# Layer 0's modulation in four 32-column tiles of TensorE, and its fourth unit in two pieces

## The chip, the core and the metric

The kernel runs on one core of a Trainium2 chip. The metric is the device time of one execution in microseconds (us). TensorE (PE) multiplies, VectorE (DVE), ScalarE (ACT) and GpSimd (POOL) do the rest, and SyncE (SP) issues most loads from the chip's memory (HBM). Each engine runs its own list of instructions in order and waits on semaphores.

## What is computed

Two decoder layers on 256 tokens of width 1024, in float32. The part that matters here is how layer 0 begins.

```python
c_act = jax.nn.silu(c)
for i in range(DEPTH):
    mod = c_act @ ada_w[i] + ada_b[i]
    sh1, sc1, g1, sh2, sc2, g2 = jnp.split(mod[:, None, :], 6, axis=-1)
    h = rms_norm(x, norm_mix[i]) * (1.0 + sc1) + sh1
    ...
    y = dilated_attention(h, attn_w_qkv[a], attn_w_out[a], ...)   # layer 0; layer 1: hgrn2_mixer
    x = x + g1 * y
    h = rms_norm(x, norm_ffn[i]) * (1.0 + sc2) + sh2
    x = x + g2 * swiglu(h, ffn_w1[i], ffn_w3[i], ffn_w2[i])
```

c is one row of 1024, ada_w[0] is 1024x6144. Of `mod` the first product needs sh1 and sc1, 2048 columns.

## The kernel before

**Products in three parts.** Weights come in units of 128x2048 (1 MB) into a ring of six slots, `raw`. ACT rounds a unit to the reduced form F32R (`whi`, `round_unit`), DVE writes the rest over the slot (`wlo`, `split_unit`), and PE adds three products: activation high x weight high, low x high, high x low. The activations stand transposed in `hT` (8 blocks of 128 columns of the model, 256 tokens), their rounded form in `hT_hi`, the rest in `hT_lo`.

**The start.** Layer 0's first six units are done by `half_unit(m)`: m is 0 to 2 with the first four blocks of hT (half 0) and 3 to 5 with the last four (half 1). So units 0 to 2 need the modulation of half 0 alone: for each half, 512 columns of sh1 and 512 of sc1. A unit is six runs of four 128x512 products: high and low part against `whi` for both tiles of tokens t, then high against `wlo` for both.

**The modulation.** ada_w's columns of a half come in eight chunks `first_w[k]`, one for 128 rows, 128x1024 each; `first_load(n)` loads chunk n, with n = 8 to 15 for half 1, into the same eight places. `first_sum(blk, k)` on DVE multiplies chunk k by the column `cact[:, k]` and adds it up in `acc[:, blk]`. PE then sums `acc` over the partitions by eight products with a column of ones (`first_reduce`); of half 0 the last chunk goes to PE directly, by eight one-column products. `first_modulation(half)` on DVE adds the bias and makes the gain `mod_a`, `first_affine(half, t)` makes h of hT in place, ACT rounds it (`first_round`), DVE makes the low part (`first_rest`).

**What sets the order.** The lists of all engines are written out by hand. SP's loads before: c, chunks 0 and 1, x, chunks 2 to 7, unit 0 in two pieces, chunk 8, unit 1, chunks 9 to 12, unit 2, chunks 13 to 15, unit 3 and on. `keep_clock(n)` runs n products whose result nobody reads, 128x512 in float32, in between (fillers, below). DVE's list for half 1 has the sums of all eight chunks around the splits of units 1 and 2. `bank[i]` are the eight banks of PSUM, where PE writes; a float32 product stands in the trace as two records with a weight load each, a float32 transpose as one.

## Time and profile before

| | us |
|---|---|
| median of 3 runs (lowest, highest) | 870.5 (870.15, 871.99) |
| the profiled execution, its own time | 872.44 |
| its span, first to last instruction | 870.6 |
| PE busy | 839.7 (96%) |
| DVE busy | 613.9 (71%) |
| ACT busy | 432.6 (50%) |
| POOL busy | 137.9 (16%) |

The times in all rows are microseconds from the start of the span, of one execution. A row of a timeline has the start, the busy time, the engine (PEld is PE's load of weights), the line, the operation, what it writes and reads, partitions x elements, and how many records it merges; in brackets the idle time ahead of it and what ended it. The end of a record of PE is modelled: it lies some 0.17 behind the end of its stream.

### The profile page before, as it was taken

Reading aid. Unit: us, or ns where it says so; the run is one execution under the profiler, and the core shown is the slowest. Engines: PE = TensorE matmul, PEld = TensorE weight load, DVE = VectorE, ACT = ScalarE, POOL = GpSimd, SP = SyncE. Lnnn points to the kernel's source line nnn. Section 1 sums busy time; section 2 is a strip of 40 time slices with the busy share of each in tenths; the row PEclk is TensorE's granted clock in tenths of the full one; section 3 lists DMA queues with packets and bytes.
Section 4 is the critical chain, followed back from the end, with each engine's and each line's share of the span. In section 5 each row is a group of like instructions: output and inputs, shape, how many; then the busy total and the mean of one; then the engine's idle time right before and its main releaser. Section 6 shows DMA issues by size and latency. Waiting matters only on the chain.

```text
span 870.6 us, 10955 instructions
## 1 busy us (share of the span) xinstructions
PE 839.7 (96%) x4254; PEld 699.8 (80%) x4254; DVE 613.9 (71%) x728; ACT 432.6 (50%) x549; POOL 137.9 (16%) x157
## 2 busy tenths in 40 slices
PE   4999999999999989999999989999999999999998
PEld 2778878878878878887888877888888788887886
DVE  4897798788888776577576676787867665654544
ACT  5355464464445555453344356778575744433431
POOL 3000101111010120011010020467813000000000
PEclk9799999999999999999999999999999999999999
DMA  9997878887877635688787745434234577665521
GB/s 320 365 357 238 293 253 276 283 255 234 284 260 235 229 108 193 198 275 293 260 271 255 240 145 180 156 98 146 97 117 129 208 248 234 228 206 180 192 96 49
DMA packets 122102, 188.97 MB, mean 217 GB/s; under 512 B 5683, under 2 KB 91048, under 8 KB 122052
## 3 DMA queue, kind: packets, MB, share of 16 engines
q1 hardware_dynamic: 109796, 146.10, 51.8%
q0 software_dynamic: 12256, 42.18, 14.4%
q8 instruction: 34, 0.56, 0.3%
q14 instruction: 16, 0.13, 0.0%
HBM read 187.18 MB, written 1.09 MB: 216 GB/s over the span
## 4 chain that ended last, share of the span: by engine, by line
PE 76%; DVE 13%; ACT 4%; issue 4%; DMA 2%; POOL 1%; SPq 0%; DVEq 0%; ACTq 0%; POOLq 0%
PE bank L526 62%; DVE wlo L1363 2%; PE bank L642 2%; DVE acc L1374 2%; DVE x L1532 2%; PE bank L722 2%; PE bank L748 1%; PE bank L916 1%; ACT whi L988 1%; PE bank L595 1%; PE bank L703 1%; PE bank L860 1%; DMA x<-in_x_dram 1%; PE bank L559 1%; DVE sq L1530 1%
## 5 line engine op out<-in xcount | busy, mean ns | idle before, releaser
L1363 DVE TENSOR_TENSOR wlo<-raw,whi 128x2048 fp32r<-128x2048 f32 x123 | 285.4, 2325 | 41.9 <-ACT whi L988 41.8
L988 ACT ACTIVATE whi<-raw 128x2048 fp32r<-128x2048 f32 (+1 forms) x124 | 235.3, 1900 | 18.9 <-DMA raw<-in_attn_w_qkv_dram 12.2
L526 PE MATMUL bank<-whi,hT_hi 128*128 128x512 f32 (+1 forms) x728 | 195.1, 391 | 2.4 <-ACT hT_hi L988 1.5
L526 PE MATMUL bank<-wlo,hT_hi 128*128 128x512 f32 (+1 forms) x752 | 194.1, 381 | 1.2 <-DVE wlo L1363 1.2
L526 PE MATMUL bank<-whi,hT_lo 128*128 128x512 f32 (+1 forms) x728 | 187.3, 380 | 0.0
L526 PEld LDWEIGHTS bank<-wlo,hT_hi 128*128 128x128 f32 x752 | 137.3, 188 | 29.5 <-DVE wlo L1363 2.0
L526 PEld LDWEIGHTS bank<-whi,hT_lo 128*128 128x128 f32 x728 | 132.9, 188 | 26.5
L526 PEld LDWEIGHTS bank<-whi,hT_hi 128*128 128x128 f32 x728 | 129.5, 188 | 29.9 <-issue 6.5
L393 POOL DMA_DIRECT2D ada_w<-in_ada_w_dram x80 | 42.7, 534 | 466.2 <-DVE acc L1374 449.0
L1374 DVE SCALAR_TENSOR_TENSOR acc<-ada_w,cact,acc 128x1024 f32<-128x1024 f32 x80 | 102.3, 1279 | 8.0 <-DMA ada_w<-in_ada_w_dram 6.0
L1224 ACT ACTIVATE arena<-bank 128x256 f32<-128x256 f32 x44 | 14.5, 381 | 166.8 <-PE bank L526 166.8
L1686 DVE TENSOR_TENSOR arena<-bank,arena 128x256 f32<-128x256 f32 x44 | 16.6, 419 | 112.2 <-ACT arena L1224 112.2
L526 PE MATMUL bank<-whi,oT_hi 128*128 128x512 f32 x240 | 70.3, 410 | 0.0
L526 PE MATMUL bank<-wlo,oT_hi 128*128 128x512 f32 x240 | 65.9, 392 | 0.0
L526 PE MATMUL bank<-whi,oT_lo 128*128 128x512 f32 x240 | 65.5, 390 | 0.0
L526 PEld LDWEIGHTS bank<-wlo,oT_hi 128*128 128x128 f32 x240 | 45.6, 190 | 10.1
L526 PEld LDWEIGHTS bank<-whi,oT_lo 128*128 128x128 f32 x240 | 45.1, 188 | 9.7
L526 PEld LDWEIGHTS bank<-whi,oT_hi 128*128 128x128 f32 x240 | 43.8, 192 | 8.0 <-issue 0.5
L988 ACT ACTIVATE oT_hi<-bank 128x512 fp32r<-128x512 f32 (+1 forms) x38 | 17.6, 464 | 58.4 <-PE bank L748 39.0
L988 ACT ACTIVATE arena<-bank 128x512 f32<-128x512 f32 (+3 forms) x63 | 30.0, 528 | 20.4 <-PE bank L526 9.2
L1131 ACT ACTIVATE arena<-arena,small 128x768 f32<-128x768 f32 (+1 forms) x16 | 12.5, 779 | 35.4 <-DVE small L1609 23.9
L399 POOL TENSOR_TENSOR wlo<-raw,spare 128x2048 fp32r<-128x2048 f32 x3 | 14.2, 4748 | 76.0 <-ACT spare L988 76.0
(184 smaller groups left out, 854.5 us busy)
## 6 DMA issues: line engine op xcount, KB each, us to landing
raw<-in_ffn_w_dram SPq DMA_DIRECT2D x88, 512.0 KB, 4.9
ada_w<-in_ada_w_dram POOLq DMA_DIRECT2D x80, 512.0 KB, 5.0
raw<-in_attn_w_qkv_dram SPq DMA_DIRECT2D x62, 512.0 KB, 6.5
raw<-in_ffn_w_dram SPq DMA_DIRECT2D x22, 1024.0 KB, 4.9
raw<-in_hgrn_w_in_dram SPq DMA_DIRECT2D x16, 1024.0 KB, 5.4
arena<-in_ada_w_dram SPq DMA_DIRECT2D x16, 512.0 KB, 10.1
raw<-in_attn_w_qkv_dram SPq DMA_DIRECT2D x4, 1024.0 KB, 7.1
raw<-in_attn_w_out_dram SPq DMA_DIRECT2D x4, 1024.0 KB, 7.4
```

What stands on the lines that cost most here:

```text
L393: pool.dma_start(ada_w[:, n % ADA_RING], a["ada_w"][layer, k * P:(k + 1) * P, b * ADA_COLS:(b + 1) * ADA_COLS]).then_inc(ada_in[n % ADA_RI ...
L399: pool.tensor_tensor(wlo[:, m % RAW, :], raw[:, m % RAW, :], hi_of(m).bitcast(F32), ALU.subtract).then_inc(s["split_second"], 1)
L526: mm = nc.tensor.matmul(dst[t][c][:, 0:n], lhs[:, k0 + k, t * P:(t + 1) * P], w[:, k, c * 512:c * 512 + n], start=start and k == 0, stop=s ...
L642: mm = nc.tensor.matmul(bank[b + t][:], lhs[:, 4 * half + k, t * P:(t + 1) * P], w[:, k, :], start=start and half == 0 and k == 0, stop=st ...
L722: mm = nc.tensor.matmul(dst, qT[:, pr % 2, g, base + qt * P:base + (qt + 1) * P], kT[:, pr % 2, g, base:base + w], start=True, stop=True)
L988: return nc.scalar.activation(dst, src, ACT.Copy)
L1131: nc.scalar.activation(pr_, pr_, ACT.Exp, bias=stat(J, 2), accum_out=stat(J, 3)).then_inc(s["att_p"], 1)
L1224: i = nc.scalar.activation(sil[:, t], gate_bank(j, t)[:, 0:FC], ACT.Silu)
L1363: nc.vector.tensor_tensor(wlo[:, m % RAW, :], raw[:, m % RAW, :], fp(hi_of(m)), ALU.subtract).then_inc(s["split"], 1)
L1374: nc.vector.scalar_tensor_tensor(out=acc[:, blk % 2], in0=ada_w[:, n % ADA_RING], scalar=cact[:, k:k + 1], in1=acc[:, blk % 2], op0=ALU.mu ...
L1532: nc.vector.tensor_tensor(x[:, t, cut], x[:, t, cut], sq[:, b % 2], ALU.add).then_inc(s["res"], 1)
L1686: i = nc.vector.tensor_tensor(hid[:, t], gate_bank(j, t)[:, FC:2 * FC], sil[:, t], ALU.mult)
```

## The change

**Sums.** Each chunk of half 0, and chunks 5 to 7 of half 1 (`SUMMED = 5`), are summed by PE: `quarters` runs four products with 32 stationary columns, all equal (`cact32`, the column of c's activation repeated 32 times, written once by DVE into a free part of `acc`), and 256 moving columns of the chunk, with outputs on partitions 0, 32, 64 and 96 of one bank. The bank adds up over the chunks. For half 1 DVE still sums chunks 0 to 4 in `acc`, and `quarters` adds that with a stationary of ones. Then DVE copies the 128x256 result to `acc`, PE transposes it in two pieces (`first_columns`), and DVE adds the bias.

**Fillers** read ones instead of x, and stand between the chunks. There are three after chunk 1, one each after chunks 2, 4 and 5 (here behind the transposes) and others, and two behind each `first_columns`.

**Unit 3** comes and is rounded in two pieces; in its products the split's run of tile 0 is moved ahead of the low part of tile 1. **Half 1's h**: DVE writes `hT_hi` of tile 0 directly and then makes h in place; ACT does both for tile 1 (`second_half_tile`).

**Order of loads**: unit 2 ahead of chunks 11 and 12; a place of a chunk is free when PE has read it (`first_mm`), not DVE. POOL's zeroing of `acc` for the next block waits for the second modulation.

```diff
@@ SP
                 blk, k = divmod(n, KC)
-                if blk and k == KC - 1:
-                    sp.wait_ge(s["first_mm"], 1)
-                elif blk:
-                    sp.wait_ge(s["first_sum"], k + 1)
+                if blk:
+                    sp.wait_ge(s["first_mm"], k + 1)
...
             first_load(KC)
             load_unit(1)
-            for n in range(KC + 1, KC + 5):
+            first_load(KC + 1)
+            first_load(KC + 2)
+            load_unit(2)
+            for n in range(KC + 3, 2 * KC):
                 first_load(n)
-            load_unit(2)
-            for n in range(KC + 5, 2 * KC):
-                first_load(n)
-            for m in range(3, UNITS):
+            load_by_halves(3)
+            for m in range(4, UNITS):
@@ PE
+            def quarters(dst, left, right, start, stop):
+
+                for r in range(4):
+                    mm = nc.tensor.matmul(dst[32 * r:32 * r + 32, 0:256], left, right[:, r * 256:(r + 1) * 256],
+                                          start=start, stop=stop)
+                return mm
+
+            def first_chunk(n, start=False, stop=False):
+
+                half, k = divmod(n, KC)
+                pe.wait_ge(first_in[n], 16)
+                mm = quarters(bank[7 if half else 3], cact32[:, k, :], first_w[k], start, stop)
+                mm.then_inc(s["first_mm"], 1)
+
+            def first_columns(half, dst):
+
+                pe.wait_ge(s["mod_copy"], half + 1)
+                for i in range(2):
+                    mm = nc.tensor.transpose(dst[:, 256 + i * P:256 + (i + 1) * P], acc[:, half, i * P:(i + 1) * P], ident[:])
+                mm.then_inc(s["mod_red"], 1)
...
+                if m == 3:
+                    pe.wait_ge(s["split"], m + 1)
+                    product(hT_hi, w[1], 0, False, True)
+                    pe.wait_ge(s["xn_lo"], 2 * half + 2)
+                    product(hT_lo, w[0], 1, False, False)
+                    product(hT_hi, w[1], 1, False, True).then_inc(s["pe_unit"], 1)
+                    return
                 pe.wait_ge(s["xn_lo"], 2 * half + 2)
                 product(hT_lo, w[0], 1, False, False)
                 if m == 2:
-                    first_reduce(1, bank[7])
+                    first_chunk(KC + SUMMED, start=True)
                 pe.wait_ge(s["split"], m + 1)
                 product(hT_hi, w[1], 0, False, True)
+                if m == 2:
+                    for k in range(SUMMED + 1, KC - 1):
+                        first_chunk(KC + k)
+                    pe.wait_ge(s["first_sum"], SUMMED)
+                    quarters(bank[7], ones[:, 0:32], acc[:, 1], False, False)
                 product(hT_hi, w[1], 1, False, True).then_inc(s["pe_unit"], 1)
+                if m == 2:
+                    first_chunk(2 * KC - 1, stop=True)
+                    first_columns(1, bank[7])
+                    keep_clock(2, 6)
@@ DVE
             def first_modulation(half):
 
+                b = bank[7 if half else 3]
+                dve.wait_ge(s["first_mm"], 2 * KC - SUMMED if half else KC)
+                nc.vector.tensor_copy(acc[:, half, 0:256], b[:, 0:256]).then_inc(s["mod_copy"], 1)
                 dve.wait_ge(s["mod_red"], half + 1)
...
-            for k in range(2, KC):
+            first_sum(1, 2)
+            first_sum(1, 3)
+            split_unit(2)
+            for k in range(4, SUMMED):
                 first_sum(1, k)
-            split_unit(2)
             first_modulation(1)
+            cut = slice(0, P)
+            for kc in range(4, KC):
+                i = nc.vector.tensor_scalar(hT_hi[:, kc, cut], hT[:, kc, cut], mod_a[:, 0, 0, kc:kc + 1],
+                                            first_shift(kc), ALU.mult, ALU.add)
+            i.then_inc(s["xn_hi"], 1)
             first_affine(1, 0)
-            first_affine(1, 1)
+            dve.wait_ge(s["h0_aff"], 3)
             first_rest(1, 0)
+            split_unit(3)
             first_rest(1, 1)
-            split_unit(3)
```

PE's list before, from the transpose of the small rows to the first product. L610 is the filler, L559 the transposes of the normalised x, L624 the table of position biases, L628 the last chunk, L603 the sum over the partitions.

```order
L616 MATMUL bank<-ident,rows 128x79
L610 MATMUL bank<-x,ident 128x512 x2
L559 MATMUL bank<-ident,arena 128x128 x8
L610 MATMUL bank<-x,ident 128x512
L559 MATMUL bank<-ident,arena 128x128 x8
L624 MATMUL bank<-arena 24x383
L610 MATMUL bank<-x,ident 128x512
L628 MATMUL bank<-cact,arena 128x1 x8
L603 MATMUL bank<-ones,acc 128x1 x8
L610 MATMUL bank<-x,ident 128x512
```

The same place after the change. L606 is `quarters`, 4 for a chunk, L627 the filler, L563 the transposes, L650 the table, L621 `first_columns`.

```order
L606 MATMUL bank<-arena,acc 32x256 x4
L627 MATMUL bank<-ones,ident 128x512
L606 MATMUL bank<-arena,acc 32x256 x4
L563 MATMUL bank<-ident,arena 128x128 x8
L627 MATMUL bank<-ones,ident 128x512
L606 MATMUL bank<-arena,acc 32x256 x4
L627 MATMUL bank<-ones,ident 128x512
L606 MATMUL bank<-arena,acc 32x256 x4
L563 MATMUL bank<-ident,arena 128x128 x8
L627 MATMUL bank<-ones,ident 128x512
L606 MATMUL bank<-arena,acc 32x256 x4
L650 MATMUL bank<-arena 24x383
L627 MATMUL bank<-ones,ident 128x512
L606 MATMUL bank<-arena,acc 32x256 x4
L621 MATMUL bank<-ident,acc 128x128 x2
```

From chunk 2 to chunk 7 the list now has five fillers between the transposes, the table and six groups of quarters, where it had two fillers and one chunk.

PE's list at the end of unit 2 before, with the sum over partitions between the low-part run and the `wlo` runs:

```order
L642 MATMUL bank<-whi,hT_hi 128x512 x4
L642 MATMUL bank<-whi,hT_lo 128x512 x4
L603 MATMUL bank<-ones,acc 128x1 x8
L642 MATMUL bank<-wlo,hT_hi 128x512 x8
L642 MATMUL bank<-whi,hT_hi 128x512 x4
```

And after the change:

```order
L664 MATMUL bank<-whi,hT_hi 128x512 x4
L664 MATMUL bank<-whi,hT_lo 128x512 x4
L606 MATMUL bank<-arena,acc 32x256 x4
L664 MATMUL bank<-wlo,hT_hi 128x512 x4
L606 MATMUL bank<-arena,acc 32x256 x4
L606 MATMUL bank<-acc,ones 32x256 x4
L664 MATMUL bank<-wlo,hT_hi 128x512 x4
L606 MATMUL bank<-arena,acc 32x256 x4
L621 MATMUL bank<-ident,acc 128x128 x2
L627 MATMUL bank<-ones,ident 128x512 x2
```

The two `wlo` runs now stand ahead of the last sum.

## Rows read from the trace of the kernel before

**Rows 1.** The page's head and first part: busy time of each engine.
```profile
span 870.6 us, 10955 instructions
PE 839.7 (96%) x4254; PEld 699.8 (80%) x4254; DVE 613.9 (71%) x728; ACT 432.6 (50%) x549; POOL 137.9 (16%) x157
```

**Rows 2.** Stretches: busy time of each engine, granted clock, DMA share, GB/s.
```profile
core 0: us, PE busy (x) PEld busy (x) DVE busy (x) ACT busy (x) POOL busy (x), PEclk, DMA share, GB/s
15.00:21.80 6.80, 6.38 (x40) 4.24 (x38) 5.97 (x11) 4.76 (x8) 0.00 (x0) 1.00 1.07 369
21.80:32.00 10.20, 9.54 (x29) 7.03 (x29) 6.80 (x15) 4.12 (x4) 1.50 (x2) 0.50 1.07 369
32.00:48.50 16.50, 16.08 (x80) 13.28 (x78) 15.59 (x19) 4.47 (x3) 1.09 (x2) 1.00 1.09 361
46.50:67.10 20.60, 19.31 (x87) 15.19 (x85) 20.26 (x31) 13.39 (x18) 0.00 (x0) 1.00 1.07 349
```

**Rows 3.** Timeline of PE, 10.9 to 22.
```profile
10.93 3.70 PE L610 MATMUL bank<-x,ident 128*128 128x512 f32 x4
...
18.79 1.12 PE L610 MATMUL bank<-x,ident 128*128 128x512 f32 x2
19.76 1.84 PE L628 MATMUL bank<-cact,arena 128*128 128x1 f32 x16
21.55 3.37 PE L603 MATMUL bank<-ones,acc 128*128 128x1 f32 x16
```

**Rows 4.** Timeline of PE, from the first unit to the second stage.
```profile
27.49 2.04 PE L642 MATMUL bank<-whi,hT_hi 128*128 128x512 f32 x4 [0.66 <-ACT hT_hi L988]
...
35.19 1.07 PE L642 MATMUL bank<-whi,hT_hi 128*128 128x512 f32 x4
36.10 1.07 PE L642 MATMUL bank<-whi,hT_lo 128*128 128x512 f32 x4
...
40.63 1.07 PE L642 MATMUL bank<-whi,hT_hi 128*128 128x512 f32 x4
...
44.26 1.84 PE L603 MATMUL bank<-ones,acc 128*128 128x1 f32 x16
...
48.46 1.17 PE L642 MATMUL bank<-whi,hT_hi 128*128 128x512 f32 x4 [0.42 <-ACT hT_hi L988]
...
67.13 1.18 PE L526 MATMUL bank<-whi,hT_hi 128*128 128x512 f32 x4 [0.89 <-DVE arena L1587]
```

**Rows 5.** Timeline of DVE, 46.1 to 67.1.
```profile
46.14 0.17 DVE L1402 TENSOR_TENSOR small<-bank,cols 128x8 f32<-128x8 f32 x1 [0.24 <-PE bank L603]
...
46.54 2.14 DVE L1411 TENSOR_SCALAR arena<-arena,mod_a,small 128x128 f32<-128x128 f32 x8
...
65.78 1.29 DVE L1587 TENSOR_TENSOR arena<-bank,small 128x512 f32<-128x512 f32 x2
```

**Rows 6.** Timeline of all engines: arrivals, the first affine, splits and roundings.
```profile
5.11 0.75 DVE L1383 TENSOR_SCALAR acc<-arena,cact 128x1024 f32<-128x1024 f32 x1 [5.11 <-DMA arena<-in_ada_w_dram]
10.01 1.06 ACT L1033 ACTIVATE sq<-x 128x1024 f32<-128x1024 f32 x1 [5.87 <-DMA x<-in_x_dram]
19.33 0.19 PEld L628 LDWEIGHTS bank<-cact,arena 128*128 128x128 f32 x1 [0.24 <-DMA arena<-in_ada_w_dram]
25.57 2.14 DVE L1411 TENSOR_SCALAR arena<-arena,mod_a,small 128x128 f32<-128x128 f32 x8
29.01 2.28 DVE L1363 TENSOR_TENSOR wlo<-raw,whi 128x2048 fp32r<-128x2048 f32 x1
42.64 1.92 ACT L988 ACTIVATE whi<-raw 128x2048 fp32r<-128x2048 f32 x1 [5.81 <-DMA raw<-in_attn_w_qkv_dram]
```

**Rows 7.** Timeline of PE around products with few stationary columns.
```profile
17.62 0.49 PE L559 MATMUL bank<-ident,arena 128*128 128x128 f32 x3
18.04 0.82 PE L624 MATMUL bank<-arena 99*24 99x383 f32 x2
...
590.25 0.70 PE L911 MATMUL bank<-arena 128*32 128x32 f32 x32
...
596.54 1.15 PE L911 MATMUL bank<-arena 128*64 128x64 f32 x16
```

**Rows 8.** Groups by line, DVE: busy, mean ns of one, idle before.
```profile
L1686 DVE TENSOR_TENSOR arena<-bank,arena 128x256 f32<-128x256 f32 x44 | 16.6, 419 | 112.2 <-ACT arena L1224 112.2
```

More of the change, by code:

```diff
@@ L309, in load_unit, with load_by_halves @@
                     sp.dma_start(slot[:, :, c0:c0 + n], src).then_inc(raw_in[m % RAW], 16)
+            def load_by_halves(m):
+                for k in range(0, 4, 2):
+                    for src, nk, c0, n in pieces(m):
+                        slot = raw[:, m, :].rearrange("p (k n) -> p k n", k=nk)
+                        sp.dma_start(slot[:, k:k + 2, c0:c0 + n], src[:, k:k + 2, :]
+                                     ).then_inc(raw_in[m] if k else s["half3_in" if m else "half_in"], 16)
             sp.dma_start(rows[0:KC, :], a["c"].rearrange("a (k d) -> (a k) d", d=P)).then_inc(s["c_in"], 16)
@@ L625, in _ @@
             keep_clock(1)
-            pe.wait_ge(first_in[KC - 1], 16)
-            for j in range(KC):
-                mm = nc.tensor.matmul(bank[3][:, KC + j:KC + j + 1], first_w[KC - 1][:, j * P:(j + 1) * P],
-                                      cact[:, KC - 1:KC], start=True, stop=True)
-            mm.then_inc(s["first_mm"], 1)
-            first_reduce(0, bank[3])
-            keep_clock(1)
+            first_chunk(7, stop=True)
+            first_columns(0, bank[3])
+            keep_clock(2)
             def half_unit(m):
@@ L1076, in _, with round_halves, second_half_tile, affine @@
             copy(tabT, bank[2][0:GH, 0:TABLE]).then_inc(s["tab_cp"], 1)
[L1077 to L1080 removed]
+            def round_halves(m):
+                act.wait_ge(s["half3_in" if m else "half_in"], 32)
+                copy(whi[:, m, 0:UNIT // 2], raw[:, m, 0:UNIT // 2]).then_inc(s["half_rounded"], 1)
+                act.wait_ge(raw_in[m], 32)
+                copy(whi[:, m, UNIT // 2:], raw[:, m, UNIT // 2:]).then_inc(s["rounded"], 1)
+            def second_half_tile():
+                def affine(dst, kc):
+                    return nc.scalar.activation(dst[:, kc, P:2 * P], hT[:, kc, P:2 * P], ACT.Identity,
+                                                bias=first_shift(kc), scale=mod_a[:, 0, 0, kc:kc + 1])
+                act.wait_ge(s["mod_ev"], 2)
+                for kc in range(4, KC):
+                    i = affine(hT_hi, kc)
+                i.then_inc(s["h0_aff_s"], 1)
+                act.wait_ge(s["h0_aff_s"], 1)
+                act.wait_ge(s["xn_hi"], 3)
+                for kc in range(4, KC):
+                    i = affine(hT, kc)
+                i.then_inc(s["xn_hi"], 1)
+            round_halves(0)
             first_round(0, 0)
@@ L1084, in _ @@
             round_unit(2)
-            round_unit(3)
-            first_round(1, 0)
-            first_round(1, 1)
+            round_halves(3)
+            second_half_tile()
             def qk_square(n):
@@ L1547, in _ @@
                                     ).then_inc(s["lbd_s"], 1)
-            for k in range(4, KC - 1):
-                first_sum(0, k)
             first_modulation(0)
```

83 lines of the change are left out of this document (38 added, 45 removed).

## The prediction, written before the kernel was run

> **What bounds the kernel now.** I read the page's first part first: TensorE (PE) is busy for 96% of the span [rows 1]. So most of what is saved or lost before the stream of products runs full reaches the end. Then I read the stretches of the first 48.5 us [rows 2], the products of PE [rows 3, 4] and VectorE (DVE) after the second modulation [rows 5]. Four things are to be seen.
>
> First, PE does no product of the layer before 27.49. It waits for the modulation of the first half: the last chunk of ada_w is there at 19.33 (the L628 weight load waits for its DMA), the eight one-column products L603, behind DVE's last sum, run from 21.55 to 24.9, DVE's small steps lead to the first affine at 25.57, and ScalarE's (ACT) rounding of the result releases PE at 27.49 [rows 3, 4, 6].
>
> Second, the granted clock is 0.50, the 1.2 GHz level, from 21.8 to 32.0, and 1.00 on both sides [rows 2]. In the last 2 us before it fell PE ran one-column products, which stream next to nothing [rows 3]. A run of four 128x512 products takes 0.91 at the full clock (35.19 to 36.10). The first unit, six such runs, takes 7.70 (27.49 to 35.19), the second 5.44 (to 40.63) [rows 4].
>
> Third, the second half: PE reaches the one-column sums L603 at 44.26, DVE has its small steps at 46.14, the first affine at 46.54, PE starts the fourth unit at 48.46 [rows 4, 5].
>
> Fourth, from 46.54 DVE never rests: affines, differences, five splits, two reductions, two normalisations, back to back to 67.07 (busy 20.26 of 20.60), and PE waits for the last of these at 67.13, 0.9 of it idle [rows 2, 4, 5]. So it is **the moment of the second half's first affine**, 46.54, that sets the stretch behind it, and the sum below is made for that moment. The loads are no bound of it: they run without a pause [rows 2], but unit 3 is there at 42.64 [rows 6] and is needed at 48.
>
> **Part 1, what one group of quarters costs.** The new unit of work is four fp32 products with 32 stationary columns and 256 moving ones, to four 32-partition pieces of a bank. A 128x512 fp32 product is two records of 0.43 (a filler: two records, 0.86) [rows 3], so a quarter is two of 0.213. One after the other the eight records are 1.71 us. Do the tiles run together? The trace has one place with 32-column tiles: the 16 products L911, whose outputs alternate between partitions 0 and 64. Their 32 records take 0.70 us with the last one's end, 22 ns each, where the 64-column form of the same line, one tile only, takes 72 ns a record (1.15 for 16) [rows 7]. A record of 32 columns streams 27 ns (0.427 x 32/512), so two tiles overlapped fully. I take the same for four: 2 x 0.213 and some 0.05 for weights and stagger, 0.48.
>
> To this comes the change of form. The table product L624 is the one small-column product between wide ones. Its first record starts 0.20 after the last transpose (three from 17.62 at 0.11 each put that at 17.84), whose stream is 0.05: 0.15 of entry. Its two records stream 0.64 (383 columns), to 18.68, the filler starts at 18.79, and takes 0.97 instead of 0.86: 0.2 of exit [rows 3, 7]. A **group between wide work is 0.15 + 0.48 + 0.20 = 0.83**. The ends: 0.48, if no change of form is paid, and 2.1, if the tiles do not overlap (1.71 + 0.05 + 0.35).
>
> The Trainium skill ("TensorEngine Tiling (Array Packing)", Key Properties) says that changing the tiling mode drains TensorE. The 0.15 before L624 agrees. This rule speaks against this change: it brings nine more such changes in and out. By the skill's "TensorE: Matmul & The Clock Gate" (Part 3) four tiles would start some 4 ns apart, which would make the group 0.79 and the sum 0.4 us lower; no row here has four tiles.
>
> **Part 2, the first half.** Chunk 0 is there at 5.11 [rows 6], chunk 1 a little behind. The quarters of both, three fillers (0.85 a record at the low clock) [rows 3] and the transpose of the small rows fill PE from 5.1 to about 11.5, with the clock risen on the way, as it had before by the filler at 18.79 (0.43 a record). The first chunk that counts, chunk 2, comes at 11.56: x was there at 10.01, chunk 7 at 19.33, so one in 1.55 us [rows 3, 6]. Behind it PE has, in order: six groups 6 x 0.83 = 5.0 (less the last exit 0.2, and 0.35 as chunk 6 and the table product follow each other in the narrow form), five fillers 4.3, sixteen transposes 1.8, the table product with its exit 0.86, and about 0.3 of waiting for chunk 3. 11.5 + 11.7 = **23.2**. So PE, not the DMA, becomes the bound: chunk 7 is 3 us old when it is summed. That is the cost of the fillers once real work shares the queue.
>
> Then the new tail: 0.2 to DVE (L603's end at 46.10 to L1402 at 46.14, and 0.17 of drain), the copy of 256 columns 0.4 (L1686 has 0.42 at this size), 0.5 for two transposes with their weight load, 0.04, two small steps of 0.2 [rows 4, 5, 8]: 1.55. First affine at 24.75 against 25.57: **0.8 gained**. ACT is ready: the table's copy and the two roundings of unit 0 (half of a 1.92 rounding each, [rows 6]) end near 24.5, and it is asked at 25.8. The first product is at 26.7. The four sums and the reduction that DVE loses were not what it waited on last; they free 8 us of DVE, which it spends idle.
>
> **Part 3, the clock.** PE is now full from 11.5 to 26.4 (two fillers cover the tail), with streams and not one-column products in its list, so I let the clock stay at 2.4 GHz. The first unit is then 5.44 and 0.25 for its split: DVE's rest and split end 3.8 after PE's start as before (27.49 to 31.29) [rows 4, 6], PE asks at 3.63. That saves 2.0 of the 7.70. PE is through four of unit 2's six runs at 26.7 + 5.7 + 5.44 + 3.63 = **41.5**, against 44.26: 2.8 earlier.
>
> **Part 4, the second half.** Here the change spends it. Before, 1.7 of L603 and 0.2 led to DVE. Now PE has, on the path: chunk 5 of the half 0.83, a run of wlo 0.91, chunk 6 0.83, the summed chunks 0.45 (same form, no change), a run of wlo 0.91, chunk 7 0.63 without exit: 4.56, to 46.05. The tail 1.55: first affine at **47.6 against 46.54, 1.06 later**. The two wlo runs stood behind the sums before, beside DVE's work; now they stand ahead of it, and two fillers stand beside DVE. DVE's five sums are done by about 41 and hide; before, DVE had all eight to add here. The loads hide: unit 2 is moved ahead of two chunks, which come by about 37, and chunk 7 by 40, all before PE asks.
>
> **Part 5, behind it.** Writing the rounded half straight from DVE saves ACT's step on the way: PE starts the fourth unit 1.15 after the first affine, 1.92 before (48.46) [rows 4]. But DVE must still make the second four affines and the difference (some 2.9), so PE waits about 0.9 for the low part, and 0.45 for the split: the unit ends about 8.0 after the first affine against 7.8 before. DVE's own list to 67.07 has the same entries: same length, 20.5. Unit 3 in two pieces costs nothing and gives nothing, as it is there 5 us early. GpSimd's memset and the ring of ada_w start 3 us later and are first needed beyond 67. So all is 1.06 later: sum 870.5 + 1.1 = **871.6**. The profiled execution had 872.4 with a span of 870.6 [rows 1], the median of the three runs is 870.5: I add the shift to the median.
>
> Each 0.1 on the group moves the end by 0.9 (six groups, then three).
>
> **Rivals.**
> A, the queue stalls on a tile: the second record of a quarter waits for the first and holds up the next tile behind it. Then a group takes five slots of 0.218, 1.44 with its changes, and the added one 0.87. Six times 0.61 in the first half, 3 x 0.61 + 0.42 in the second, 0.4 from the early chunks: 6.4 more, **878**. It decides the sign from a group of 0.9 on. L911's 22 ns speaks against it, but it has two tiles only. With no overlap at all (2.1) it is 886.
> B, faster: the change of form is free and only the streams count, 0.48. PE then waits for chunks 2 and 3, the first affine is at 23.6, the second half's at 45.5: 1.05 gained, **869.4**. If ACT or DVE also lose waits behind it (PE's 0.9 at 67.13) or the tail is 0.5 shorter, 868.5. L624's gaps speak against it.
> C, the clock falls all the same between 12 and 32, since quarters and transposes stream less than full products: 2.3 or more lost in one stretch, **874**.
> D, the relief of DVE is no relief, and nothing else moves: the forecast itself. That the sum is done on PE and off DVE is seen in the order; it can't fail to be done.
>
> **How the numbers follow.** Forecast 0.55, A with its worse form 0.15, B 0.2, C 0.1. The forecast's own range, for groups of 0.7 to 1.0, is 870.3 to 873.2. The range given is 868.2 to 876.5: B and C whole, A outside. What a measurement of this kernel can tell from no change is about 0.2%, 1.7 us. Of the forecast's 0.55 about two thirds lie within it. Faster 0.17, same 0.40, slower 0.43.
>
> **What would show it.** Right: quarters' records at under 60 ns apart, chunk 7's group ending near 23, products from 26.7 at clock 1.00, first affine of the second half near 47.6 with PE full from 41 to 46 and DVE idle before it, then 20.5 us of unbroken DVE. Wrong: groups of 1.1 or more (A), a clock of 0.50 after 12 (C), DVE with gaps between 47 and 67 (then Part 5 fails), or PE waiting for chunks (B).

## The result, and the profile after

| | before | after |
|---|---|---|
| median of 5 (lowest, highest), us | 870.5 (870.15, 871.99) | 875.7 (871.2, 876.58) |
| ratio with its 95% interval | | 1.0045 (1.0029 to 1.0061) |
| the profiled execution, its own time | 872.44 | 871.2 |
| its span | 870.6 | 869.4 |

The changed kernel is slower, by 3.9 us by the ratio and by 5.2 between the medians, where 1.1 was forecast. The range held the time, the likeliest value was 4.1 too low. (One execution each of two kernels below, half1 and keep_after, ran at a mean granted clock of 0.56 and took 1422 and 1435 us; they are left out.) And the profiled execution of the changed kernel is shorter than that of the kernel before, while its median is longer. One execution of each would have shown the change as a gain.

The page's head and first part for the changed kernel, to set beside [rows 1]:

```profile
span 869.4 us, 11083 instructions
PE 842.1 (97%) x4320; PEld 692.3 (80%) x4320; DVE 603.0 (69%) x720; ACT 435.0 (50%) x556; POOL 137.7 (16%) x157
```

DVE has lost 10.9 us of work and PE has gained 2.4, and neither tells what the end did. So I went by the moments that the prediction names. Timeline of PE from chunk 0 to the first product (L606 quarters, L627 filler, L563 transposes, L650 the table, L621 the two transposes of the sum), to set beside [rows 3]:

```profile
5.05 1.08 PE L606 MATMUL bank<-arena,acc 128*32 128x256 f32 x8 [2.63 <-DMA arena<-in_ada_w_dram]
...
11.87 0.64 PE L606 MATMUL bank<-arena,acc 128*32 128x256 f32 x8
12.44 1.13 PE L627 MATMUL bank<-ones,ident 128*128 128x512 f32 x2
13.50 0.64 PE L606 MATMUL bank<-arena,acc 128*32 128x256 f32 x8
14.07 1.09 PE L563 MATMUL bank<-ident,arena 128*128 128x128 f32 x8
...
22.29 0.64 PE L606 MATMUL bank<-arena,acc 128*32 128x256 f32 x8
23.48 0.44 PE L621 MATMUL bank<-ident,acc 128*128 128x128 f32 x2 [0.55 <-DVE acc L1450]
23.75 1.89 PE L627 MATMUL bank<-ones,ident 128*128 128x512 f32 x4
26.27 1.17 PE L664 MATMUL bank<-whi,hT_hi 128*128 128x512 f32 x4 [0.63 <-ACT hT_hi L1026]
```

The four tiles do run together: eight records, two to a quarter, are over in 0.64 with the last one's modelled end, and within the group the first records of the four quarters start 6 to 7 ns apart (13.500, 13.506, 13.513, 13.520). The next wide operation starts 0.57 behind the group's first record (13.50 to 14.07), and a group behind a filler starts 0.20 later than the filler's stream of 0.86 ends (12.44 to 13.50). So a group costs 0.77.

Timeline of PE in the second half, to set beside [rows 4]:

```profile
41.26 0.64 PE L606 MATMUL bank<-arena,acc 128*32 128x256 f32 x8
41.83 1.20 PE L664 MATMUL bank<-wlo,hT_hi 128*128 128x512 f32 x4
42.95 0.64 PE L606 MATMUL bank<-arena,acc 128*32 128x256 f32 x8
43.41 0.61 PE L606 MATMUL bank<-acc,ones 128*32 128x256 f32 x8
43.95 1.19 PE L664 MATMUL bank<-wlo,hT_hi 128*128 128x512 f32 x4
45.08 0.64 PE L606 MATMUL bank<-arena,acc 128*32 128x256 f32 x8
...
68.02 1.20 PE L530 MATMUL bank<-whi,hT_hi 128*128 128x512 f32 x4 [0.86 <-DVE arena L1645]
```

And of DVE: the copy of the sum, which it waits 5.44 for, and the first affine (L1619), to set beside [rows 5]:

```profile
45.78 0.42 DVE L1450 COPY acc<-bank 128x256 f32<-128x256 f32 x1 [5.44 <-PE bank L606]
46.74 0.17 DVE L1456 TENSOR_TENSOR small<-bank,cols 128x8 f32<-128x8 f32 x1 [0.53 <-PE bank L621]
...
47.13 1.23 DVE L1619 TENSOR_SCALAR hT_hi<-arena,mod_a,small 128x128 fp32r<-128x128 f32 x4
```

The second half's first affine is at 47.13 against 46.54, and the seventh unit starts at 68.02 against 67.13 [rows 4, 5]: 0.89 later. That is nearly what the sum said (1.06). From that start to PE's last product this execution takes 797.1. The changed kernel's other timed executions have spans of 872.6 to 874.8 and a mean granted clock of 0.991 to 0.995, where the profiled one has 1.000. So the missing time had to be looked for in executions that the first profile did not show.

### The profile page after: what moved, and what is told of

It reads as the page before. It is cut to its first block, busy times and chain, and to the rows that moved or that the text cites. A ratio compares the mean times of both kernels' runs of the same rounds, so it can differ in the third digit from the quotient of the medians.

```text
span 869.4 us, 11083 instructions
## 1 busy us (share of the span) xinstructions
PE 842.1 (97%) x4320; PEld 692.3 (80%) x4320; DVE 603.0 (69%) x720; ACT 435.0 (50%) x556; POOL 137.7 (16%) x157
## 4 chain that ended last, share of the span: by engine, by line
PE 77%; DVE 12%; ACT 4%; issue 4%; DMA 1%; POOL 1%; SPq 0%; DVEq 0%; ACTq 0%; POOLq 0%
PE bank L530 61%; PE bank L664 3%; DVE wlo L1420 2%; DVE acc L1431 2%; DVE x L1586 2%; PE bank L786 1%; ACT whi L1026 1%; PE bank L760 1%; PE bank L954 1%; PE bank L599 1%; PE bank L898 1%; PE bank L627 1%; PE bank L741 1%; DVE sq L1584 1%; DMA ada_w<-in_ada_w_dram 1%
```

## The experiments

**The changed kernel again, and three edits on its start.** First the changed kernel once more, then single parts of it taken out.

again: no edit.

> The changed kernel once more, nothing altered. Its first profile had TensorE's granted clock at 1.00 over the whole span and 869.4 us; its other runs took 872.6 to 874.8 at a mean clock of 0.991 to 0.995. Theory (clock): the spread over its runs is stretches at the low clock, so the span again follows the mean clock, some 869 at 1.00 and 874 to 875 at 0.991, and the profile shows stretches at 0.50 where TensorE has gaps. Rival (something else, loads or DVE): spans differ by 3 us or more at the same mean clock.

nofill:

```diff
             first_chunk(2)
-            keep_clock(1)
             first_chunk(3)
...
             first_chunk(4)
-            keep_clock(1)
             first_chunk(5)
```

(and three more, all that stand between chunk 2 and chunk 7).

> The changed kernel without the five fillers between chunk 2 and chunk 7 (the three after chunk 1 and those behind the transposes of the sums stay). Theory (the fillers delay the sum): TensorE is done with chunk 7 near 19.9 instead of 22.9, the first affine comes near 21.5, the first product at 24.3, where the rounding of unit 0 ends (it waits for its loads), 2 us earlier than 26.3, and all of it reaches the end if the clock stays: 2 us faster. Rival (they are needed for the clock): the granted clock falls to 0.50 before or in the first units, which costs 2 us or more, and it is the same or slower.

behind:

```diff
-                product(hT_hi, w[1], 1, False, True).then_inc(s["pe_unit"], 1)
                 if m == 2:
                     first_chunk(2 * KC - 1, stop=True)
+                product(hT_hi, w[1], 1, False, True).then_inc(s["pe_unit"], 1)
+                if m == 2:
                     first_columns(1, bank[7])
```

> The changed kernel with the second wlo run of unit 2 moved behind chunk 7's quarters. Theory (the path to the second half's first affine sets the stretch behind): quarters and copy are 0.9 to 1.1 earlier, the first affine at 46.1 instead of 47.1, TensorE resumes after the first normalisations at 67.0 instead of 68.0, 1 us faster in all. Rival (TensorE's own work is the bound there): the run only changes its place and nothing is gained.

half0, where the first half keeps its quarters and the second has DVE's eight sums and eight one-column products (the main lines; the quarters, the transposes and the two fillers of the second half are gone with them):

```diff
                 if m == 2:
-                    first_chunk(KC + SUMMED, start=True)
+                    pe.wait_ge(s["first_sum"], KC)
+                    for j in range(KC):
+                        mm = nc.tensor.matmul(bank[7][:, j:j + 1], acc[:, 1, j * P:(j + 1) * P], ones[:, 0:1],
+                                              start=True, stop=True)
```

> The changed kernel with half 1 undone: DVE sums all eight chunks of the second half and TensorE reduces them by eight one-column products between the low-part run and the wlo runs of unit 2; half 0, fillers, unit 3 in pieces stay. Theory (half 0 gains, half 1 spends it): the first product at 26.3 as in the changed kernel, DVE ends its sums near 44.6, first affine of the second half near 47.0, so the same as the changed kernel within 0.5 us: what TensorE does for half 1 is worth nothing. Rival (half 1's quarters are the cost): the first affine comes at 45 and it is 2 us faster than the changed kernel.

| | ratio (interval) | median | span, median | clock, median | first product | 2nd half's affine | seventh unit |
|---|---|---|---|---|---|---|---|
| before, alongside | | 870.07 | 868.3 | 0.993 | | | |
| again | 1.0062 (1.0050 to 1.0074) | 875.14 | 873.4 | 0.993 | 26.67 | 47.51 | 68.41 |
| nofill | 1.0022 (1.0011 to 1.0033) | 871.99 | 870.1 | 0.995 | 22.97 | 44.38 | 65.54 |
| behind | 1.0041 (1.0025 to 1.0057) | 873.8 | 871.9 | 0.993 | 26.64 | 46.63 | 67.50 |
| half0 | 1.0047 (1.0031 to 1.0064) | 873.8 | 872.0 | 0.994 | 26.03 | 46.71 | 67.85 |

(Columns 4 and 5 are of the timed executions, columns 6 to 8 of the profiled one.)

Against the changed kernel's two ratios nofill is 2.0 to 3.5 us faster (2 expected) and behind 0.3 to 1.8 (1 expected). The ten timed executions of the changed kernel follow their mean clock, as again's first theory said: a span of 869.4 at 1.000, 872.6 at 0.995 and 0.996, 872.8 to 873.9 at 0.993 and 0.994, 873.4 to 875.1 at 0.990 to 0.992. In behind, the one execution at 1.000 has a span of 868.0, the median is 871.9.

The fillers between the chunks cost 2.9 at the seventh unit (68.41 to 65.54; 2.5 against the changed kernel's first profile). In nofill PE takes chunk 7 at 18.28, which is 4.0 earlier than the changed kernel, and in its profile the clock stays at 1.00 without them, so they bought nothing there. What PE waits for is now ACT (1.23 ahead of the first product), as the timeline shows:

```profile
18.28 0.73 PE L606 MATMUL bank<-arena,acc 128*32 128x256 f32 x8
19.58 0.44 PE L621 MATMUL bank<-ident,acc 128*128 128x128 f32 x2 [0.57 <-DVE acc L1445]
19.85 1.89 PE L627 MATMUL bank<-ones,ident 128*128 128x512 f32 x4
22.97 1.17 PE L659 MATMUL bank<-whi,hT_hi 128*128 128x512 f32 x4 [1.23 <-ACT hT_hi L1021]
```

The second run of wlo ahead of chunk 7 costs 0.9: from the first quarters of the second half to the affine it is 5.87 in the changed kernel (41.26 to 47.13) and 4.98 in behind (41.65 to 46.63).

In half0 PE is back at the sums at 41.1 and waits for DVE, which has eight sums to do, in all to 44.2:

```profile
44.31 1.83 PE L694 MATMUL bank<-ones,acc 128*128 128x1 f32 x15 [3.21 <-DVE acc L1438]
```

So the quicker first half is worth nothing while DVE sums the second, and the second half's own edit spends what it wins. But nofill starts the seventh unit 1.6 **earlier** than the kernel before did in its profile, and is 0.2% slower than it. No term of the start explains that. (Its profiled execution, at a mean clock of 0.999, has a span of 868.2; the median of its twelve is 870.1, at 0.995.)

**Where the rest goes.** In the second profile of the changed kernel I read stretch after stretch for the granted clock (columns as in [rows 2]), and found five of 3.41 us each at 0.50, each behind a place where PE waits, transposes or runs one-column products:

```profile
194.00:198.00 4.00, 3.49 (x30) 3.12 (x28) 3.97 (x5) 3.72 (x6) 0.00 (x0) 1.00 0.82 258
198.30:201.50 3.20, 3.20 (x9) 2.45 (x8) 3.20 (x4) 0.80 (x3) 0.53 (x1) 0.50 0.95 305
249.00:252.70 3.70, 1.71 (x12) 1.30 (x11) 3.59 (x7) 1.58 (x4) 1.58 (x3) 1.00 0.86 299
252.90:256.10 3.20, 3.20 (x9) 2.53 (x8) 3.10 (x3) 2.17 (x2) 0.55 (x1) 0.50 0.93 326
322.00:324.40 2.40, 1.07 (x9) 1.08 (x10) 1.94 (x8) 0.34 (x2) 0.00 (x0) 1.00 0.84 341
324.60:327.80 3.20, 3.20 (x9) 2.49 (x8) 1.83 (x5) 3.01 (x7) 0.00 (x0) 0.50 0.00 0
520.00:522.40 2.40, 0.63 (x6) 0.63 (x7) 1.52 (x6) 0.55 (x3) 0.00 (x0) 1.00 1.02 377
522.60:525.80 3.20, 3.20 (x10) 2.62 (x9) 1.92 (x5) 2.62 (x7) 0.00 (x0) 0.50 0.03 11
...
546.50:549.70 3.20, 3.20 (x11) 2.71 (x10) 2.80 (x2) 2.22 (x4) 0.00 (x0) 0.50 0.65 250
```

The first such place in that execution (PE's timeline): transposes, a wait for DVE of 0.51, transposes, and sixteen records of one column (L599). The clock falls at 198.2, within the run of four that takes 1.54 here; the next run takes 1.71 (198.95 to 200.66), where one takes 0.91 at the full clock:

```profile
194.08 0.82 PE L769 MATMUL bank<-ident,arena 128*128 128x128 f32 x6
195.41 0.66 PE L741 MATMUL bank<-ident,arena 128*128 128x128 f32 x4 [0.51 <-DVE arena L1645]
195.90 1.84 PE L599 MATMUL bank<-ones,acc 128*128 128x1 f32 x16
197.61 1.54 PE L530 MATMUL bank<-whi,hT_hi 128*128 128x512 f32 x4
```

The first profile of the same kernel has the same list at the same place, and the full clock behind it:

```profile
198.00:201.30 3.30, 3.30 (x17) 2.69 (x16) 3.30 (x3) 0.51 (x2) 0.53 (x1) 1.00 0.95 306
252.00:255.30 3.30, 3.30 (x17) 2.72 (x16) 2.30 (x3) 0.71 (x1) 0.55 (x1) 1.00 0.98 284
```

Product by product the second profile falls 5.2 behind the first after 68 us, nearly all of it in these places: 1.6 across the first, 1.6 the second, 1.2 the third, nothing the fourth, and at the fifth 1.6, of which PE's next waits take back 1.2. nofill's profile has none, behind's has the same five, half0's has one at 46.1 and one at 517. The profile of before had two (318.8 and 516.7), which I had not looked for:

```profile
318.80:322.10 3.30, 3.30 (x13) 2.91 (x13) 1.93 (x7) 1.55 (x4) 0.00 (x0) 0.50 0.12 46
516.80:520.10 3.30, 3.00 (x11) 2.77 (x12) 2.00 (x6) 1.00 (x3) 0.00 (x0) 0.50 0.34 133
```

**Is it the full clock at the start, or the changed work?** The kernel before loses its low stretch at the start whatever it does later. So its start was warmed (to keep the clock at 1.00 there), and the changed kernel's was made cold again.

warm (all its fillers read ones):

```diff
+            keep_clock(6, 3)
...
             mm.then_inc(s["first_mm"], 1)
+            keep_clock(1)
             first_reduce(0, bank[3])
-            keep_clock(1)
+            keep_clock(2)
```

> Edit: the kernel before, with fillers alone added at the start, so that the granted clock does not fall to 0.50 there. Six fillers stand behind the transpose of c's row, and the chunk that goes straight to PE and the sum over partitions have one filler between them and two behind (all read ones). Nothing of the change is in it. What both theories expect of the start: clock 1.00 from about 10.5 on, the sum over partitions of the first half in 1.8 instead of 3.37, first product near 26.5 (27.49 before), unit 0 in 5.9 instead of 7.7, the second half's first affine near 46.6 since DVE's eight sums set it, the seventh unit's start at 67.2 to 67.9 (67.13 before). Theory 1, that low stretches of 3.41 late in the program come with a start at the full clock: two to five of them behind 68, clock 0.990 to 0.996, spans 870 to 874 and a median of 872 or more, though nothing of layer 0's modulation is changed. Theory 2, that they come with the changed work itself, or the cold start only hides in the mean: none to two of them as before, spans 867 to 869.5, clock 0.996 or more, median 869 to 870.

half1 (the first half as in the kernel before, DVE's seven sums, one chunk and the sum on PE as one-column products, and its fillers; the main lines):

```diff
-            first_chunk(7, stop=True)
-            first_columns(0, bank[3])
-            keep_clock(2)
+            for j in range(KC):
+                mm = nc.tensor.matmul(bank[3][:, KC + j:KC + j + 1], first_w[KC - 1][:, j * P:(j + 1) * P],
+                                      cact[:, KC - 1:KC], start=True, stop=True)
...
+            pe.wait_ge(s["sum0"], KC - 1)
+            for j in range(KC):
+                mm = nc.tensor.matmul(bank[3][:, j:j + 1], acc[:, 0, j * P:(j + 1) * P], ones[:, 0:1],
```

> Edit: the changed kernel with half 0 undone. DVE sums chunks 0 to 6 of half 0, the last chunk and the sum over partitions go to PE as one-column products, with before's fillers, so the start is cold again; half 1 has the quarters, the order of loads and the fourth unit of the change. Expected by my prediction's steps: first product near 27.5 with the clock at 0.50 from about 22 to 32, PE at the first group of half 1 near 44.3, from there 4.0 to the end of chunk 7's group and 1.4 to the affine: 49.7 to 50.2, and the seventh unit's start near 70.5 to 71. So 3.4 to 3.9 more than before by this term alone. Theory 1 (late low stretches come with a full clock at the start): none to two of them, as before, span 871.5 to 874.5, median 873.5 to 876. Theory 2 (they come with the quarters or the new order): three to five, spans 875 to 879, median 877 to 880.

nofill_behind: both edits from above.

> Edit: the changed kernel without the five fillers between chunks 2 and 7 of half 0, and with the second run against wlo of unit 2 behind chunk 7's quarters instead of ahead of it. By the two single runs (2.9 from the fillers at the seventh unit's start, 0.5 to 0.9 from the run) the first product comes at 23.0, the second half's first affine near 43.8 to 44.2 and the seventh unit starts at 64.6 to 65.1, 2.0 to 2.5 ahead of the kernel before. Theory 1 (late low stretches depend on a full clock at the start): two to four in most executions, spans 868 to 872, median 870.5 to 872, no better than before though it is 2 us ahead at 68. Theory 2 (chance of each program's own): the median is 868 to 869.5 and faster than before.

before2: no edit of the kernel before.

> Edit: none, the kernel before once more, for the places of its low stretches of 3.41. Both theories expect the start as in the first profile (0.50 from about 22 to 32, the seventh unit's start at 67.1). Theory 1: none to two late low stretches, and where there is one it stands in one of the five places where the changed kernel had them (behind PE's waits near 195, 249, 319, 517 and 541). Theory 2, that they stand anywhere: other places than these. Span 867.4 to 870.6, ratio 1.000.

| | ratio (interval) | median | span, median | clock, median | 2nd half's affine | seventh unit |
|---|---|---|---|---|---|---|
| before, alongside | | 870.74 | 868.95 | 0.992 | | |
| warm | 1.0015 (1.0004 to 1.0026) | 872.17 | 870.3 | 0.993 | 45.62 | 67.14 |
| half1 | 1.0035 (1.0022 to 1.0049) | 873.29 | 871.5 | 0.992 | 47.99 | 68.87 |
| nofill_behind | 1.0026 (1.0013 to 1.0040) | 873.01 | 871.2 | 0.992 | 43.17 | 65.05 |
| before2 | 1.0009 (1.0000 to 1.0018) | 871.51 | 869.7 | 0.990 | 44.89 | 66.04 |

before2 gives three things. The same kernel measured 1.0009 against itself, so 0.1% is not to be read from these ratios. Its low stretches stand at 317.3 and 515.3, in the same two places as in the first profile, as its stretches show:

```profile
23.80:30.50 6.70, 5.34 (x12) 3.80 (x12) 6.50 (x13) 3.06 (x3) 0.91 (x2) 0.50 1.06 378
317.40:320.60 3.20, 3.20 (x12) 2.81 (x11) 1.92 (x6) 1.72 (x5) 0.00 (x0) 0.50 0.09 35
515.40:518.60 3.20, 3.13 (x12) 2.84 (x13) 1.77 (x6) 1.12 (x3) 0.00 (x0) 0.50 0.29 110
```

And its seventh unit is 1.1 earlier than in the execution that the prediction was built on. x was there at 9.65, not 10.01 [rows 6], with which the sum over the partitions starts 0.35 earlier; and the clock fell at 23.7 for 6.8, not at 21.8 for 10.2 as in [rows 2], so that this sum took 1.95 instead of 3.37 [rows 3]:

```profile
21.20 1.95 PE L603 MATMUL bank<-ones,acc 128*128 128x1 f32 x16
...
66.04 1.19 PE L526 MATMUL bank<-whi,hT_hi 128*128 128x512 f32 x4 [1.47 <-DVE arena L1587]
```

warm starts the seventh unit where the first profile of before did (67.14) and still has four late low stretches, at 46.5, 196.7, 319.6 and 517.6, where before2 has two. Its 0.15% is 1.3 us; 1.1 of that stand at the seventh unit by before2's start, none by the first profile's. That leans to theory 1, which had two to five of them and a median of 872 or more. half1 has a cold start, one late stretch (517.2), and its 0.35% is about what its late seventh unit says (2.8 behind before2's). That also fits theory 1. (Its start came some 2 earlier than expected, the affine at 47.99 and not near 50, with a cold stretch of 6.8 and not 10.) nofill_behind starts the seventh unit at 65.05, as expected, and yet is slower than either theory had it: four late low stretches in its profile, at 247.7, 319.3, 517.3 and 541.2.

The mean clocks of the timed executions can be read as a count. A stretch of 3.41 at 0.50 takes 0.002 off the mean clock (the profiled execution of again: five, 0.990). By this estimate, if the executions start as their profiles do, warm has 3.9 of them in an execution (mean 0.9923), the changed kernel 3.4 (0.9934 over its ten), and the other three kernels of the first table 2.6 to 3.8. half1 and the kernel before have 4.3 and 3.9 to 4.9, but 2.7 of those are the cold start (that is what keep_before, below, has without late stretches: 0.9947). That leaves 1.6 late ones for half1 and 1.2 to 2.2 for the kernel before. So the late stretches seem to go with the start at the full clock, with the change or without it. That is theory 1, by an estimate and not by a direct count. What they cost is the next question, since warm, with as many of them as the changed kernel, is only 0.15% slower.

half1 shows the price of the second half's own edit: PE reaches the first group at 42.12, and the affine follows 5.87 later, at 47.99, as in the changed kernel, where the kernel before needed 2.28 (44.26 to 46.54 [rows 4, 5]).

**Holding the clock.** The test that does settle whether the late stretches carry the loss takes them away: fillers in the five places, mostly inside PE's waits, in both kernels alike (`hold` is the filler, n times, into bank b).

```diff
+            def hold(n, b):
+                for _ in range(n):
+                    nc.tensor.matmul(b[:], ident[:], ones[:, 0:1].to_broadcast([P, 512]), start=True, stop=True)
...
             def norm_t(q, t):
+                if q in (1, 2) and t == 0:
+                    hold(2, bank[4])
...
-                pe.wait_ge(s["qk_norm"], n + 1)
+                if n < 3:
+                    pe.wait_ge(s["qk_norm"], n + 1)
                 if n >= 3:
                     pe.wait_ge(s["qk_tev"], 2 * n + which)
+                    if (n, which) == (7, 0):
+                        hold(1, qk_bank(n, which))
+                    if (n, which) == (9, 0):
+                        hold(2, qk_bank(n, which))
+                    pe.wait_ge(s["qk_norm"], n + 1)
...
                     reduce_task(HGRN_TASK)
+                    hold(1, bank[4])
```

> Edit: the changed kernel with eight fillers more (ones, into banks that nobody reads until they are written anew), in the five places behind which its low-clock stretches stood: one ahead of the transposes of q and k near 195, two near 249, two each ahead of the transposes of the normalised x near 319 and 516, one behind the sum over partitions near 540. By their 0.86 and the waits that they stand in (0.52, 2.00, 2.31, 2.41, 0.35) they cost 0.35 near 195, 0.5 near 540 and nothing else: 0.85. If the low stretches explain what the changed kernel's runs lose over its profiled execution (span 869.4, none of them), then they are gone here: clock 0.998 to 1.000, spans 869.5 to 870.8 in nearly all executions, median 871.3 to 872.6, so 3 to 4 less than the changed kernel has, though more work is done. If something else makes those runs long (the loads, or chance), the clock or the fillers change nothing: spans 872.6 to 875.5, median 875.5 to 876.5.

> Edit: the kernel before with the same eight fillers in the same five places. Its cold start stays (0.50 from about 22, for 6.8 or 10.2). Its two late low stretches (near 317 and 515, 1.1 and 0.6 lost) go, the fillers cost 0.85, so it gains 0.8 in an execution that had both: spans 867.5 to 869.5, clock 0.994 to 0.996, median 869.5 to 870.5, ratio 0.998 to 1.000. With both kernels held, what is left between them is the start alone: 0.9 where the cold stretch is 10.2 long, 2.0 where it is 6.8. If instead the held ones still differ by 4 or more, the late low stretches are not what the change lost.

> Edit: the same eight fillers in the changed kernel without the five fillers between chunks 2 and 7 of the first half. Its profile had no late low stretch: span 868.2, seventh unit at 65.5, 1.2 of its 2.5 given back at 298, where DVE waits 3.0 for ada_w. Expected: 868.2 + 0.85, spans 868.6 to 869.8, clock 0.997 to 1.000, median 870.5 to 871.3; so 1.2 less than the held changed kernel, not the 2.5 by which it starts the seventh unit earlier. If the give-back is not there (the loads do not bound it), 2.5 less.

keep_both (the same eight fillers in nofill_behind):

> Edit: the held kernel without the five early fillers (the eight fillers in the five places stay), and the second run against wlo of unit 2 behind chunk 7's quarters. It should start the seventh unit at 65.0, 0.5 ahead of the held one without this edit. If what is gained at 68 beyond about 1.2 is given back at 298, because DVE waits near 288 for ada_w, the last product comes within 0.2 of that kernel's and the median is 869.5 to 870.4. If the gain goes through, both are 0.5 less: 869.4 or less, and the fastest of all kernels here.

| | ratio (interval) | median | before, alongside | span, median | clock, median | seventh unit |
|---|---|---|---|---|---|---|
| keep_after | 1.0022 (1.0010 to 1.0033) | 872.26 | 870.54 | 870.1 | 1.000 | 67.67 |
| keep_before | 0.9989 (0.9978 to 1.0000) | 869.62 | 870.54 | 867.8 | 0.995 | 66.23 |
| keep_nofill | 0.9991 (0.9979 to 1.0003) | 869.92 | 870.54 | 868.1 | 1.000 | 65.45 |
| keep_both | 0.9994 (0.9982 to 1.0007) | 870.53 | 871.62 | 868.8 | 0.998 | 65.24 |

The first place in keep_after, PE's timeline and the stretches, to set beside the same place in again:

```profile
193.70 1.02 PE L558 MATMUL bank<-ones,ident 128*128 128x512 f32 x2
194.57 0.60 PE L754 MATMUL bank<-ident,arena 128*128 128x128 f32 x4
195.00 1.84 PE L606 MATMUL bank<-ones,acc 128*128 128x1 f32 x16
196.71 1.18 PE L530 MATMUL bank<-whi,hT_hi 128*128 128x512 f32 x4
```

```profile
194.00:198.00 4.00, 4.00 (x28) 3.35 (x27) 4.00 (x4) 3.59 (x5) 0.00 (x0) 1.00 0.87 273
198.00:201.30 3.30, 3.30 (x16) 2.75 (x15) 3.12 (x3) 0.51 (x2) 0.53 (x1) 1.00 0.94 299
```

In keep_after the late low stretches are gone: the clock is 0.999 or 1.000 in all its executions but the one left out, and the changed kernel comes down from 1.0045 and 1.0062 to 1.0022, though it does eight fillers more. The kernel before gains too, but 0.1%. So the late stretches cost the changed kernel 0.2 to 0.4%, some 2 to 3.5 us, and the kernel before about 1. What is left between the two held kernels is 0.33%, 2.9 us (2.3 between their median spans); their profiles have 1.4 of that at the seventh unit and 1.7 at the last product.

nofill comes down from 1.0022 to 0.9991 by the same fillers, 2.7 us. It is 2.3 below the held changed kernel, about its lead of 2.2 at the seventh unit, where 2.5 was expected if the lead goes through and 1.2 if not; but of these two profiles' lead only 1.4 is left at the last product. It and keep_before are 0.1% below the kernel before, which these intervals barely tell from nothing.

keep_both starts the seventh unit 0.2 earlier than keep_nofill, not 0.5, and its median of 870.53 is above both values expected of it (the kernel before, alongside, was 1.1 higher here than beside the other three). Its twelve executions say why: the eight fillers do not hold the clock in all of them. Six have a mean clock of 0.999 or 1.000 and a median of 869.6, six have 0.997 or 0.998 and one of 871.6. The expectation that the wait of DVE for ada_w near 288 gives gains back did not hold as a rule: against the changed kernel's first profile PE lost 1.2 there in nofill, where that wait is 3.0, and 0.1 to 0.2 in keep_nofill and keep_both, where it is 2.1 and 2.0. None of these kernels beats the kernel before by more than 0.1%.

## Why the prediction was right or wrong

**Part 1, the group.** Right. 0.77 where the sum had 0.83, between wide work. The streams of four tiles overlap as those of two did in [rows 7] (0.46 from one group to the next in the same form, 42.95 to 43.41; the sum had 0.48 and 0.45), and a change of form in and out costs 0.20 and 0.11, where it had 0.15 and 0.20, so that part of the agreement is two errors that offset. Rivals A and B, the stall of the queue and the free change, fall with that. The remark under A that the sign turns from a group of 0.9 on does not follow from the sum: at 0.9 us of the end for each 0.1 of the group it turns at 0.71. The Trainium skill ("TensorE: Matmul & The Clock Gate", Part 3) has the tiles start about 4 ns apart. The trace has 6 to 7 ns. The prediction's estimate of 0.79 from it is near the measured 0.77, though no closer in the stream itself (0.44 by the estimate, 0.46 measured).

**Part 2, the first half.** Right in kind, 0.4 off. DVE starts to copy at 23.00, so chunk 7 is summed at about 22.8, not 23.2, since nothing was waited for at chunk 3 and the groups were a little cheaper, though chunk 2 was summed 0.4 later than assumed (11.87). The tail is 1.55 as worked out: first affine 24.35, first product 26.27 (24.75 and 26.7). The remark that PE and its fillers become the bound here was right and should have been taken further: without the fillers the first product comes 3.3 earlier.

**Part 3, the clock at the start.** Right. The stretches of the changed kernel, to set beside [rows 2]:

```profile
12.00:23.00 11.00, 10.93 (x76) 4.17 (x72) 1.03 (x9) 7.55 (x13) 0.00 (x0) 1.00 1.06 359
23.00:48.50 25.50, 23.77 (x116) 15.61 (x117) 18.53 (x29) 9.18 (x11) 1.45 (x2) 1.00 1.08 364
```

From the first product to the first group of the second half 15.0 us pass (14.8 in the sum). Rival C, which looked for the low stretch between 12 and 32, did not come. What it never asked is whether the clock falls anywhere else.

**Part 4, the second half.** Right: 5.87 from the first group to the affine, where the sum had 6.1, and the affine 0.59 later than in the profile of before, 1.06 in the sum. The order of the second wlo run is 0.9 of it.

**Part 5, behind it.** The step that failed is its last sentence, "So all is 1.06 later". Up to the seventh unit it holds (0.89), with one slip: DVE's list is not of the same length, 20.9 from affine to unit and not 20.6. Of these 0.3, 0.24 lie ahead of DVE's last split: 1.36 from the start of the reduction to the split (62.44 to 63.80), 1.12 before (61.79 to 62.91). DVE waits there until ACT has rounded the unit, as the profile of again names it:

```profile
62.83 1.21 DVE L1632 TENSOR_REDUCE small<-sq 128x8 f32<-128x1024 f32 x1
64.19 2.29 DVE L1420 TENSOR_TENSOR wlo<-raw,whi 128x2048 fp32r<-128x2048 f32 x1 [0.15 <-ACT whi L1026]
```

Two terms were missing.

First, the base. The sum put the shift from one profiled execution on the median of others. That execution's seventh unit was 1.1 later than before2's and 0.9 later than keep_before's. In keep_before the cold stretch is as long, 10.2 from 21.3 on, but x was there at 9.12 and not at 10.01, and the sum over the partitions starts 0.9 earlier; in before2 x was 0.36 earlier and the cold stretch shorter. Against these the changed kernel's seventh unit (67.67 to 68.41) is 1.4 to 2.4 later. The prediction saw that this execution had 872.4 against a median of 870.5 and did not ask where the 1.9 lay.

Second, the late low stretches. They are not in the sum at all. With them held off, the changed kernel is 1.9 us above the kernel before as it stands, instead of 3.9 and 5.4 in two measurements. The page's clock row in 40 slices does not show one of 3.41 in a slice of 21.8 (9 stands for anything from 0.90 up), which is how I passed over the two in the profile of before.

**The rivals and the chances.** D was no rival but the forecast itself: DVE is idle for 5.4 us ahead of the second half's sum and nothing comes of it, as it said. Slower had 0.43 and came, but by a cause that no rival named; much of its weight lay on a queue that stalls. That the range held 875.7 is luck: the forecast's own range ended at 873.2, and the room above it was left for C, the low clock between 12 and 32, which did not come.

**Still open.** Why the changed kernel meets more of the late stretches than the kernel before is not settled. The same list of instructions at the same place ran at 1.00 in one execution and at 0.50 in another. warm and the count from the mean clocks lean to their coming with a start at the full clock, without any of the change; why they would is open. All variants with quarters in the first half lose more than their seventh unit accounts for (nofill is 0.5 to 1.6 earlier there than the profiles of the kernel before, and 0.22% slower), while warm, with as many late stretches, loses 0.15%. What ties the one to the other was not tried.

## What to carry to other kernels

Read the granted clock over the whole program, not only in the stretch that a change touches, and in more than one execution: a stretch of low clock behind a thin place of PE may be there in one execution and not in the next, and five of them outweighed the whole change. Where PE waits 2 us for a partner, a dummy product inside that wait cost nothing here and kept the products behind it at full rate, in every execution of keep_after and keep_nofill that is counted and in half of those of keep_both; where PE has work of its own, each filler is a cost (five of them cost 2.2 to 2.9 at the seventh unit here and bought nothing that a run shows). Add a predicted shift to a median only after asking what made the profiled execution differ from it.

## What the runs showed of the hardware

Four 32-column tiles of float32, two records each, run together: 0.46 for the eight from group to group, the four starts 6 to 7 ns apart, with 0.2 for the entry from wide work and 0.1 for the way back.

In again the granted clock falls to 0.50 for 3.41 us behind a stretch in which PE waits and transposes (PE busy 0.63 of 2.40 ahead of the one at 522), and also behind one in which it was busy for 3.49 of 4.00, with transposes and one-column products in it (198). Across the first two it costs 1.6 us each, and nothing in the end across the one at 522. The same code at the same place had it in one execution and not in another.
